# Expert weights of gate and down loaded as whole rows, with the steps of an expert, the opening and one decay product reordered

## What is computed

```python
h = rmsnorm(x, norm_mix[i]); u = h @ w_in          # opening: first product of the kernel

# gated linear attention: log decays of each token, forward and backward
la = jax.nn.log_sigmoid(jnp.einsum('bsnr,nrc->bsnc', z, w2) + b2) / GLA_TAU

# experts: each of 16 takes its top 96 tokens (64 of the prompt, 32 of the sample)
xe = hf[idx]
hid = jax.nn.silu(jnp.einsum('ecd,edf->ecf', xe, wg)) * jnp.einsum('ecd,edf->ecf', xe, wu)
ye = jnp.einsum('ecf,efd->ecd', hid, wd) * gate[..., None]
out = jnp.zeros_like(hf).at[idx.reshape(-1)].add(ye.reshape(-1, D))
```

## Time and profile before

| | us |
|---|---|
| median of 3 runs | 2899.19 (2898.5 to 2904.4) |
| the profiled execution | 2901.71 |
| its span, first to last instruction | 2899.6 |
| busy: PE / PEld / DVE / ACT / POOL | 2796.0 / 2262.4 / 2002.7 / 1593.6 / 316.7 |
| expert loads, gate + up + down | 256 + 256 + 256 of 512 KB |

### The profile page before, as it was taken

One profiled execution on the slowest core, in us unless ns is written; L12 is line 12 of the kernel. 1 busy time (PEld: TensorE's weight loads), 2 busy tenths in 40 slices (PEclk: granted clock), 3 DMA queues, 4 the chain that ended last, 5 costly groups with the idle time before them and its releaser, 6 DMA issues.

```text
span 2899.6 us, 44178 instructions
## 1 busy us (share of the span) xinstructions
PE 2796.0 (96%) x15216; PEld 2262.4 (78%) x15216; DVE 2002.7 (69%) x2596; ACT 1593.6 (55%) x2268; POOL 316.7 (11%) x309
## 2 busy tenths in 40 slices
PE   8999999999899999997999999999998999999978
PEld 7998988888777766665899989888886777666656
DVE  4148874476599988887541579644755998888874
ACT  3324343243488887877432333432534888777764
POOL 1031000033100110000010300000421100000000
PEclk9999999999999999999999999999999999999989
DMA  6122232165599999999230212221746999999981
GB/s 191 37 55 65 67 87 67 59 200 178 201 355 372 371 374 374 374 374 358 94 91 25 75 57 70 84 77 59 221 164 227 360 371 374 374 374 374 374 297 51
DMA packets 375179, 605.43 MB, mean 209 GB/s; under 512 B 20076, under 2 KB 140748, under 8 KB 374928
## 3 DMA queue, kind: packets, MB, share of 16 engines
q1 hardware_dynamic: 362864, 563.81, 55.6%
q0 software_dynamic: 12192, 39.93, 5.4%
HBM read 547.04 MB, written 56.62 MB: 208 GB/s over the span
## 4 chain that ended last, share of the span: by engine, by line
PE 77%; DMA 9%; DVE 7%; issue 3%; ACT 3%; DVEq 1%; SPq 0%; ACTq 0%; POOLq 0%
PE PS L1855 19%; PE PS L1826 15%; PE PS L1828 15%; PE PS L1827 15%; DMA raw<-in_w_down_e 8%; PE PS L1806 3%; PE PS L1950 2%; ACT whi L816 1%; DVE wlo L1255 1%; PE PS L1939 1%; PE PS L2043 1%; DVE flo L1260 1%; PE PS L2167 1%; PE PS L2057 1%; DVE zacc L1408 1%
## 5 line engine op out<-in xcount | busy, mean ns | idle before, releaser
L1255 DVE TENSOR_TENSOR wlo<-raw,whi 128x1024 fp32r<-128x1024 f32 (+2 forms) x872 | 1040.6, 1222 | 362.7 <-ACT whi L816 347.2
L816 ACT ACTIVATE whi<-raw 128x1024 fp32r<-128x1024 f32 (+2 forms) x872 | 899.8, 1047 | 379.2 <-PE PS L1828 267.4
L1855 PE MATMUL PS<-hT,fhi 128*128 128x512 f32 (+1 forms) x2048 | 451.2, 342 | 0.6
L1826 PE MATMUL PS<-whi,xeT 128*96 128x512 f32 x1024 | 406.2, 397 | 9.6 <-DVE wlo L1255 6.5
L1828 PE MATMUL PS<-whi,xeT 128*96 128x512 f32 x1024 | 404.4, 395 | 0.0
L1827 PE MATMUL PS<-wlo,xeT 128*96 128x512 f32 x1024 | 402.0, 393 | 0.0
L1826 PE MATMUL PS<-whi,hT 128*128 128x432 f32 (+1 forms) x960 | 361.3, 376 | 2.1 <-DVE wlo L1255 2.1
L1827 PE MATMUL PS<-wlo,hT 128*128 128x432 f32 (+1 forms) x960 | 356.8, 372 | 0.0
L1828 PE MATMUL PS<-whi,hT 128*128 128x432 f32 (+1 forms) x960 | 356.7, 372 | 0.0
L1855 PEld LDWEIGHTS PS<-hT,fhi 128*128 128x128 f32 x2048 | 315.3, 189 | 43.4 <-issue 1.3
L1855 PE MATMUL PS<-hT,flo 128*128 128x512 f32 (+1 forms) x1024 | 262.9, 338 | 0.0
(11 more groups left out here) (282 smaller groups left out, 3619.3 us busy)
## 6 DMA issues: line engine op xcount, KB each, us to landing
raw<-in_w_gate_e SPq DMA_DIRECT2D x256, 512.0 KB, 11.2
raw<-in_w_up_e SPq DMA_DIRECT2D x256, 512.0 KB, 11.6
raw<-in_w_down_e SPq DMA_DIRECT2D x256, 512.0 KB, 12.6
raw<-in_w_in SPq DMA_DIRECT2D x64, 512.0 KB, 4.3
raw<-in_w_in SPq DMA_DIRECT2D x48, 432.0 KB, 5.4
gate_logits<-raw SPq DMA_DIRECT2D x32, 384.0 KB, 2.7
gate_logits<-fout SPq DMA_DIRECT2D x32, 384.0 KB, 2.7
gates<-gate_logits SPq DMA_DIRECT2D x32, 384.0 KB, 5.5
```

The costliest lines, as they stand in the source:

```text
L816: A(whi[slot % SPLIT][:, 0:w], raw[slot][:, 0:w], ACT.Copy).then_inc(s_hi, 1)
L1255: V.tensor_tensor(wlo[j % SPLIT][:, 0:w], raw[j % slots][:, 0:w], whi[j % SPLIT][:, 0:w].bitcast(F32), ALU.subtract).then_inc(s_lo, 1)
L1826: nc.tensor.matmul(out, x[0], w[0], start=first, stop=False)
L1855: m = nc.tensor.matmul(PS[:, bb, 0:(t1 - t0) * 128], w[wn], x[xn](t0, t1), start=first and p == 0, stop=last and p == 2)
```

## The change

Four edits:

- **Loads.** Gate's steps 0 to 7 and down's steps 16 to 23 take 128 rows and all 1024 columns each, so that a row of the transfer is 4 KB and a step's block is contiguous in memory. Up's steps 8 to 15 keep 256 rows of 512 columns. Number, size and buffers of the loads stay.
- **Steps of an expert.** Gate comes whole (each step feeds banks 0 and 1), then up by halves (banks 2 and 3), then down whole (banks 4 and 5). Both Silu stand at step 7, the multiplies at steps 11 and 15, the transposes of the first half of `sil` after step 13, both `ye` copies at step 23.
- **Opening.** Tile 0 is normalised, transposed and split ahead of tile 1; tile 1's transposes on TensorE stand between the third and the fourth step of tile 0's product.
- **Decay product.** In tiles 1 to 5 the first of 8 pieces of the gate step moves ahead of the wait for `zlT`.

```diff
@@ -607,11 +607,12 @@
-                    if s < 16:
-                        fetch(s % RING, (wg_f, wu_f)[s // 4 % 2], l * (NE * D) + e * D + s % 4 * 256, 2, s // 8 * 512, 512)
+                    if s < 8:
+                        fetch(s % RING, wg_f, l * (NE * D) + e * D + s * 128, 1, 0, FF)
+                    elif s < 16:
+                        fetch(s % RING, wu_f, l * (NE * D) + e * D + s % 4 * 256, 2, s // 4 % 2 * 512, 512)
                     else:
-                        j = s - 16
-                        fetch(s % RING, wd_f, l * (NE * FF) + e * FF + (j // 4 * 512 + j % 2 * 256), 2, j // 2 % 2 * 512, 512)
+                        fetch(s % RING, wd_f, l * (NE * FF) + e * FF + (s - 16) * 128, 1, 0, D)
@@ -889,13 +890,16 @@
             warm(ACT.Sqrt)
-            for t in range(2):
-                act.wait_ge(s_xin[t], 16)
-                norm_square(0, T_N0, t)
-                root(t)
-                w_hi(0, t)
+            act.wait_ge(s_xin[0], 16)
+            norm_square(0, T_N0, 0)
+            root(0)
+            w_hi(0, 0)
             norm_hi(0, T_N0, 0)
+            w_hi(0, 1)
             w_hi(0, 2)
+            act.wait_ge(s_xin[1], 16)
+            norm_square(0, T_N0, 1)
+            root(1)
             w_hi(0, 3)
@@ -1152,11 +1156,11 @@
                         j = l * TPL + e * 4 + (T_E + 2)
-                        if s in (3, 11):
-                            c = s // 8
+                        if s == 7:
                             act.wait_ge(s_used, done)
-                            A(sil[:, c * 512:(c + 1) * 512], PS[0:CAP, c, :], ACT.Silu).then_inc(s_sil, 1)
-                        if s == 11:
+                            for c in range(2):
+                                A(sil[:, c * 512:(c + 1) * 512], PS[0:CAP, c, :], ACT.Silu).then_inc(s_sil, 1)
+                        if s == 13:
                             t_hi(j, hidT[0][:, 0:4, :], tbank(0, 4, CAP))
@@ -1164,11 +1168,11 @@
                             t_hi(j + 3, xeT[0][:, 4:8, :], tbank(1, 4, CAP))
-                        if s in (21, 23):
-                            c = (s - 21) // 2
+                        if s == 23:
                             wait_alone(act, s_used, done)
-                            A(ye[:, c * 512:(c + 1) * 512], PS[0:CAP, 4 + c, :], ACT.Copy,
-                              scale=gateT[:, bass.ds(e, 1)]).then_inc(s_y, 1)
+                            for c in range(2):
+                                A(ye[:, c * 512:(c + 1) * 512], PS[0:CAP, 4 + c, :], ACT.Copy,
+                                  scale=gateT[:, bass.ds(e, 1)]).then_inc(s_y, 1)
                         n = (s + 4) % RING
@@ -1307,11 +1311,12 @@
-            for t in range(2):
-                norm_out(0, 0, t)
-                w_lo(0, t)
+            norm_out(0, 0, 0)
+            w_lo(0, 0)
             norm_lo(0, T_N0, 0)
+            w_lo(0, 1)
             w_lo(0, 2)
+            norm_out(0, 0, 1)
             w_lo(0, 3)
@@ -1720,13 +1725,13 @@
                         j = l * TPL + e * 4 + (T_E + 2)
-                        if s in (7, 15):
-                            c = s // 8
+                        if s in (11, 15):
+                            c = (s - 11) // 4
                             dve.wait_ge(s_used, l * SPL + e * ES + (S_E + s + 1 + SPLIT))
...
                             V.tensor_tensor(h, h, PS[0:CAP, 2 + c, :], ALU.mult).then_inc(s_hid, 1)
-                        if s == 11:
+                        if s == 13:
                             t_lo(j, hidT[1][:, 0:4, :], tbank(0, 4, CAP), hidT[0][:, 0:4, :])
@@ -1868,7 +1873,6 @@
             norm_t(0, 0, T_N0, 0, xnb[:, 0, :])
-            norm_t(0, 0, T_N0, 1, xnb[:, 1, :])
             for l in range(DEPTH):
@@ -1876,7 +1880,13 @@
                     pe.wait_ge(*normed(l, T_N0, t))
-                    chunk(l * SPL, CW, u_free, [t], t == NT - 1)
+                    if l == 0 and t == 0:
+                        for j in range(3):
+                            step(j, j, CW, 2 * j, [0], j == 0, False, u_free, False)
+                        norm_t(0, 0, T_N0, 1, xnb[:, 1, :])
+                        step(3, 3, CW, 6, [0], False, True, u_free, False)
+                    else:
+                        chunk(l * SPL, CW, u_free, [t], t == NT - 1)
                     if t + 2 < NT:
@@ -1995,9 +2005,8 @@
                                              la[:, m, d * 256:(d + 1) * 256], start=True, stop=True)
-                    if n == 0:
-                        gate_step(l, F_GLA, 0, 3)
                     if n < NT:
+                        gate_step(l, F_GLA + n, 0, 1 if n else 3)
                         pe.wait_ge(s_zl, l * NT + n + 1)
@@ -2006,7 +2015,7 @@
                     if n < NT:
-                        gate_step(l, F_GLA + n, 0 if n else 3, 6)
+                        gate_step(l, F_GLA + n, 1 if n else 3, 6)
                         branch_transposes(branch_units(n)[0])
@@ -2218,38 +2227,48 @@
-                def expert_steps(e, s0, n, bank, x, k0, first, last):
+                def half_steps(e, s0, n, bank, k0):
...
                             kk = k0 + 2 * j + k
-                            m = product(PS[0:CAP, bank, :], (x[0][:, kk, :], x[1][:, kk, :]), (w[0][:, k, :], w[1][:, k, :]),
-                                        first and j == 0 and k == 0, last and j == n - 1 and k == 1)
+                            m = product(PS[0:CAP, bank, :], (xeT[0][:, kk, :], xeT[1][:, kk, :]), (w[0][:, k, :], w[1][:, k, :]),
+                                        kk == 0, kk == KT - 1)
+                        m.then_inc(s_used, 1)
+
+                def row_steps(e, s0, k0, n, bank, x):
+
+                    for kk in range(k0, k0 + n):
+                        pe.wait_ge(s_lo, l * SPL + e * ES + (S_E + s0 + kk + 1 + RAW))
+                        for c in range(2):
+                            m = product(PS[0:CAP, bank + c, :], (x[0][:, kk, :], x[1][:, kk, :]),
+                                        [x_[(s0 + kk) % SPLIT][:, c * 512:(c + 1) * 512] for x_ in (whi, wlo)],
+                                        kk == 0, kk == KT - 1)
                         m.then_inc(s_used, 1)
...
                     pe.wait_ge(s_tlo, tl)
-                    for c in range(2):
-                        expert_steps(e, 8 * c, 4, c, xeT, 0, True, True)
-                        if c == 1:
-                            pe.wait_ge(s_hid, l * 32 + e * 2 + 1)
-                            transposes(None, 0, [sil[:, k * 128:(k + 1) * 128] for k in range(4)], (s_tlo, tl), CAP)
-                        expert_steps(e, 8 * c + 4, 4, 2 + c, xeT, 0, True, True)
+                    row_steps(e, 0, 0, KT, 0, xeT)
+                    half_steps(e, 8, 4, 2, 0)
+                    half_steps(e, 12, 2, 3, 0)
+                    pe.wait_ge(s_hid, l * 32 + e * 2 + 1)
+                    transposes(None, 0, [sil[:, k * 128:(k + 1) * 128] for k in range(4)], (s_tlo, tl), CAP)
+                    half_steps(e, 14, 2, 3, 4)
                     pe.wait_ge(s_tlo, tl + 1)
-                    expert_steps(e, 16, 2, 4, hidT, 0, True, False)
+                    row_steps(e, 16, 0, 2, 4, hidT)
                     pe.wait_ge(s_hid, l * 32 + e * 2 + 2)
                     transposes(None, 1, [sil[:, k * 128:(k + 1) * 128] for k in range(4, 8)], (s_tlo, tl), CAP)
-                    expert_steps(e, 18, 2, 5, hidT, 0, True, False)
+                    row_steps(e, 16, 2, 2, 4, hidT)
                     pe.wait_ge(s_ga, l * (17 * 16) + e * 16 + 32)
...
                     pe.wait_ge(s_tlo, tl + 2)
-                    expert_steps(e, 20, 2, 4, hidT, 4, False, True)
+                    row_steps(e, 16, 4, 2, 4, hidT)
                     transposes(None, 1, [xe[:, k * 128:(k + 1) * 128] for k in range(4, 8)], (s_tlo, tl + 2), CAP)
-                    expert_steps(e, 22, 2, 5, hidT, 4, False, True)
+                    row_steps(e, 16, 6, 2, 4, hidT)
```

## The result

| | before | after |
|---|---|---|
| median, us | 2898.85 (2898.42 to 2904.4, 4 runs) | 2874.17 (2873.47 to 2874.68, 4 runs) |
| ratio, 95% interval | | 0.9911 (0.9898 to 0.9923) |
| the profiled execution, span, us | 2901.71, 2899.6 | 2874.68, 2872.6 |
| packets of the DMA queues | 375179 | 309643 |

The account below looks back on a forecast made before the run. TensorE was taken to bound early experts (34.70 us), DMA late ones (35.80). -20.2 + 1.1 - 6.6 + 0.3 = -25.4 us gives 2876.3 against the profiled execution, 2873.8 from the median; range 2869.7 to 2888.5.

Parts of the forecast that it names:

- the lead: Expert loop: the ring of 12 buffers starts ahead; six experts 1.10 us faster than their data use up some 6.9 us.
- Part 1: Expert loops: whole rows for gate and down let all 16 experts go at 34.70 us, -20.2 us for both layers.
- the price of a 4 KB load: Expert loop: taken as 1.26 us, against 1.355 for 2 KB rows, so the DMA needs 34.3 us per expert.
- the sum is robust: Expert loop: with the lead spread over 15 experts, a DMA need of 35.16 us (1.314 us per 4 KB load) still suffices.
- The order of the steps: Expert loop: gate, then up, then down brings two waits closer, but all covers stay positive; costed at nothing in the loop.
- the walk's cover: Expert loop: ScalarE and VectorE followed through an expert; first half of `sil` times up ready with 0.7 us to spare.
- The tail's +1.1: End of a layer: nothing hides the second `ye` copy before the last scatter, about 0.57 us each, +1.1 for two layers.
- Part 2: Gated linear attention rounds: gate matmuls moved ahead of the wait for `zlT` fill it in five of six rounds, -6.6 us.
- Part 3: Opening: first product 3.9 us earlier, but tile 2 ready at 20.6 to 23.9 against 21.98; -1.4 to +1.9, taken as +0.3 us.
- (a): Rival, expert loop: HBM or the destination sets the rate, so the rows bring nothing; 2894.0 us, chance 0.09.
- (b): Rival, expert loop: 4 KB loads reach only 396 GB/s, 1.325 us, need 35.3; -15.2 for -20.2, 2879 us, chance 0.10.
- (c): Rival, expert loop: the first half's multiply comes late, TensorE stalls 1.2 us per expert, +38 us, 2912 us; chance 0.09.

Follow-up runs that it names:

- fewer_before: The kernel before with the third product (low part of activations by high part of weights) left out in down, 16 of 144 matmuls per expert: 2899.30 us, against 2899.46.
- halves_both: The kernel after, new step order kept, with gate and down loaded as half rows (256 rows of 512 columns) again: 2897.34 us.
- halves_down: The kernel after with only the loads of down back to half rows (256 rows of 512 columns), gate still whole rows: 2879.72 us.
- fewer_rows: The kernel after with the third product (low part of activations by high part of weights) left out in down, 16 of 144 matmuls per expert: 2862.01 us.
- late_twice: The kernel after with two extra VectorE subtractions, on data nothing uses, ahead of the first multiply of each expert: 2923.75 us.
- fewest_rows: The kernel after with the third product (low part of activations by high part of weights) left out in gate, up and down, 96 matmuls per expert: 2874.42 us.

## Why the prediction was right, and where it wasn't

**What bounds the loop** was read rightly: TensorE early (fewer_before), DMA late (halves_both), the lead between them (halves_down).

**Part 1, -20.2.** From the first to the last scatter the two layers lost 530.16 - 519.39 = 10.8 and 531.06 - 519.40 = 11.7 us, 22.4 together. 20.2 of it is the late experts' distance from 34.70, as forecast; the other 2.2 come from the early rhythm itself, 34.63 and not 34.70 (30 distances of 0.07), which nothing in the working foresaw.

The step that failed is the price of a 4 KB load. It was taken as 1.26 us, from the rate in 4 us of the residual rows, for a need of 34.3. The landings of the same six loads give another price. The first is issued at 686.00 us and the last at 688.6; the shortest and the longest time to landing belong to these two:

```profile
L527 SPq DMA_DIRECT2D rows<-in_x_sample x2: 432/432/433, 688.1 to 688.6; - x2
...
DMA to landing us min/median/max: 7.6/9.4/11.4
```

So they land from 693.6 to 700.0 us, five distances of 1.28 us, 410 GB/s, and the loop has the same price (fewer_rows above). The window of 4 us holds about three loads, and its single us read 410 to 438 GB/s: it could not tell 1.25 from 1.28. With 1.28 the prediction's own sum gives 16 x 1.28 + 8 x 1.355 + 3.3 = 34.62; the 0.13 up to 34.75 no run places. The time came out as forecast because a shortage of 0.12 us or less is far below what the lead covers. But "the sum is robust" was too strong: at its break-even need of 35.16 halves_down lost 5.5 us. The lead isn't one number: 6.9 us where experts lacked 1.1 us each, 5.4 to 5.7 where they lacked 0.5. Why, no run shows.

**The order of the steps** costs nothing in the loop, as costed; the walk's cover of 0.7 us was 0.75. The tail's +1.1 came, as 1.2: from ScalarE's last copy into the tile `pp`, ahead of the loop, to the first scatter, after takes 0.6 us longer in each layer than before.

**Part 2, -6.6.** Between before and after the rounds gave 3.1 us in layer 0 and 3.6 in layer 1, 6.7 together; undone, 7.1. With one wait left, the matmuls' waits of layer 0 fell by 3.3 - 1.0 = 2.3 us and those of the weight loads by 5.7 - 1.3 = 4.4. The gain lies between the two, as the prediction took it; neither measure alone gives it.

**Part 3, +0.3.** Right in mechanism, too small: +0.85 in the trace of after (tile 3's transposes come that much later than before) and +1.5 over all traces, both within -1.4 to +1.9. What the prediction left out of the sum as an "if", that the clock falls with the new wait, came in eight of nine traces.

**The rivals.** (a) fell with 386 to 387 GB/s in the loop. The 358 GB/s of the Trainium skill (page "DMA: Bandwidth & Descriptors", section "Where 436 GB/s comes from") don't bind here in any expert, where the whole rows alone moved the rate from 374 to 387. (b) had the direction of the error right, but not the size: 1.28 us and not 1.325, and its loss needs a need well above 34.75. The 2% estimated there from the Trainium skill (page "DMA: Bandwidth & Descriptors", section "Why small descriptors are slow (HBM only)") is too little, and the 8% set beside it too much: from 1.355 to 1.28 us is 6%, alone and in the loop. (c) has the right price (a second subtraction that takes 1.13 us cost 1.14, in every expert), and its condition didn't occur. Its counter-argument, VectorE's 3 us of idle time, was worth nothing: late_twice stalls TensorE with that time still there.

**The sum.** In the spans -27.0 us, against -25.4; the parts add up to -22.4 + 1.2 - 6.7 + 0.85 = -27.1. The medians differ by 24.7, since the profiled execution of before stood 2.9 us above its median and that of after 0.5. That the median came within 0.4 us of the forecast is in part luck: the 2.2 us of part 1 that the working did not foresee and the 2.3 us between spans and medians nearly cancel.

## What to carry to other kernels

Where two limits lie within a few per cent, find the second one by taking work off the first, before and after the change: the loop of after shows no wait for loads, and yet its DMA is up to 0.12 us per expert too slow, covered by a lead; the time from issue to landing, which creeps up, tells of it. Take the price of a load from the distances between landings, over several loads, and not from the rate of a short window. The cover of a wait is not the idle time of the engine that it waits for: measure it by adding a known operation ahead of it. And a wait in a dense stretch of TensorE can cost twice, once itself and once by the clock after it (here in eight of nine traces); order ScalarE's work so that the next tile's rows are ready first.

## What the chip showed that was not expected

fewest_rows leaves out 32 more matmuls per expert than fewer_rows and is slower, 2874.42 against 2862.01 us. Its early experts swing between 30.2 and 43.7 us. In the first distance of layer 0, 42.8 us, the granted clock is 1.00, then 0.88, then 0.64, and the DMA share falls to 0.71, where it is 1.03 to 1.06 in the other windows shown (windows of 826 to 869 us):

```profile
826.00:840.00 14.00, 14.00 (x51) 6.92 (x49) 14.00 (x13) 13.77 (x16) 10.82 (x1) 1.00 1.04 398
840.00:855.00 15.00, 7.25 (x33) 4.18 (x32) 11.31 (x13) 6.96 (x9) 8.24 (x3) 0.88 1.03 389
855.00:869.00 14.00, 9.47 (x35) 6.59 (x36) 5.93 (x6) 6.97 (x10) 0.09 (x1) 0.64 0.71 236
```

TensorE stood idle for half of the middle window and a third of the last, 10.8 us in one wait for the next expert's tokens `xe`. Their gather stands behind the scatter and an index copy on GpSimd, and these took 10.82 and 7.16 us, against 1.50 and 1.00 in the same place in after:

```profile
PE PS L1811 <- DMA xe<-h_rows,idx_g: 10.8, 1, 10.8
```

```profile
826.12 10.82 POOL L791 DMA_INDIRECT x_res<-ye,idx_s  x1 [29.11 <-ACT ye L1174]
844.19 7.16 POOL L781 COPY idx_s<-idxT 96x1 uint32 x1 [7.25 <-DMA x_res<-ye,idx_s]
...
852.46 0.95 POOL L787 DMA_INDIRECT xe<-h_rows,idx_g  x1 [0.98 <-issue]
```

VectorE was busy for all of the 14.00 us in which the scatter began; whether that slows GpSimd no run tests. While TensorE waited, its clock fell, and SP waited up to 11.3 us for a free buffer.

With the same opening, the first rise of the clock came 3.5 to 5.5 us after the first product, in the nine traces.

A load of 4 KB rows cost 1.28 us both by itself and in a loop with gathers, scatters and 2 KB rows, 6% less than one of 2 KB rows. And TensorE's dense rhythm of an expert was 34.70 us in before, 34.71 in halves_both, 34.65 in halves_down and 34.63 in after, with the same matmuls: it fell as more of the loads came in whole rows. The cause is open.
